# Layer 1's modulation moved from matrix products in layer 0's attention to VectorE row sums in layer 0's MLP

## The chip, the core and the metric

One core of one Trainium2 chip runs the whole program. The metric is the device time of one execution in microseconds; lower is better. All numbers are float32.

## The reference

Two blocks run one after the other on 256 latent tokens of width 1024. The first block has two layers, which also carry 256 context tokens through layer 0. Cut to what matters here:

```python
silu_c, silu_ctx = silu(c), silu(c_ctx)              # 1024 each
for l in range(2):
    mod_lat = silu_c @ w_ada[l] + b_ada[l]           # 1024 x 6144 weights
    mod_ctx = silu_ctx @ w_ada[l] + b_ada[l]
    sh1, sc1, gt1, sh2, sc2, gt2 = split(mod_lat, 6)
    h = rms_norm(x, g_attn[l]) * (1 + sc1) + sh1     # then projections and
    ...                                              # two attentions ("mla", "na")
    x = x + gt1 * gated_merge(...)
    h2 = rms_norm(x, g_mlp[l]) * (1 + sc2) + sh2
    x = x + gt2 * squared_relu(h2 @ w_ff1[l]) @ w_ff2[l]
```

The second block ("hybrid_layer", twice) projects its own norm of x, runs four mixers, and reads a memory `mem` of 256 rows, normed over its width: `rmsnorm(mem, mem_norm_g) @ w_mem_kv`. The memory depends on nothing that the first block computes.

## The kernel before

Features lie on the 128 partitions and tokens in the free dimension, so a 1024 x 256 activation is eight tiles. Each engine has its instructions written out by hand in one order; semaphores join them, and nothing is reordered at run time. Helpers of the same name (`modulation`, `softmax`, `split_weights`) stand once in each engine's block.

**Weights.** `weight_entries` lists every weight tile in the order of use; `weight_chunks` packs them into chunks of up to 2048 columns (1 MB), and SP streams the chunks through `ring`, five slots of 1 MB (L849). Chunks of the merge, output and MLP products are "split": ScalarE writes a rounded high part (L947), VectorE the difference (L1276), into `w_parts`, and TensorE makes three products for each pair of tiles (L427 to L429). Split chunks use ring slots 0 to 2 only, since a buffer of the parts lies over slots 3 and 4; `ring_slots` gives each chunk the slot after the one of the chunk before it, modulo 3 or 5. When a non-split chunk after a split stretch falls in slot 3 or 4, SP waits until TensorE is through with the last split chunk, and all later chunks wait behind it:

```python
if not split and i and slot >= RAW:
    ended = [j for j in range(i) if slots[j][0]]
    if ended:
        sp.wait_ge(*event(*chunk_used(ended[-1])))
```

**Modulation.** The first third of layer 0's is made by TensorE at the start: two columns (silu of c and of c_ctx) are stationary, and 256 columns of w_ada move, 8 products for each of 8 steps (L523), a copy by ScalarE, two transposes, two additions by VectorE. The rest of layer 0's are row sums of VectorE (`row_block`, L1306): w_ada's columns lie on partitions, and a scalar_tensor_tensor over 1024 elements multiplies them with a broadcast silu row (`c_rows`) and accumulates into `mod_sum`; two such instructions, one for c and one for c_ctx, make a block of 128 outputs. All 24 steps of layer 1's modulation are TensorE's, one after every other score tile of layer 0's attention (`modulation_step`, `next_modulation`): each takes one ring chunk.

**Attention.** Layer 0 has four groups of 16 tiles (8 heads times 2 halves): mla and na (512 keys, four key tiles), mlac and nac (context queries, 256 keys, two key tiles), in the order mla, mlac, na, nac. Layer 1 has mla and na only. A tile is a score product (L600), a maximum (L1251), an Exp (L915), a scaling (L1257), transposes (L504), a copy (L909), and for each head, a pair of tiles, a value product (L607). Stages are three tiles apart (AHEAD). In the na group the tiles 4 to 11 also carry the split of h into `h_parts` (ScalarE L1045, VectorE L1282), over 512 tokens in layer 0 and 256 in layer 1, and a bias addition (L1250).

**MLP.** Four groups; in each, eight ff1 tiles and eight ff2 tiles, each 24 products. VectorE takes the relu (L1528), the low part (L1282), the residual (L1492). A weight chunk holds two tiles. Layer 0 moves 512 tokens, layer 1 moves 256. The memory is squared in layer 0's group 1 (its sum on TensorE is L456 between groups 1 and 2), normed in group 2 and multiplied with its gain in layer 1's group 0.

**Block 2** starts with three `memk` tiles (L445), a norm of x, and `dt` (L685), then a long run of projections.

Of the kernel before, what the change touches and what calls it, by code (L numbers as in the profile page):

```python
# [35 lines left out]
ALU = mybir.AluOpType  # L36
# [3 lines left out]
P = 128  # L40
# [31 lines left out]
def weight_entries():  # L72
# [12 lines left out]
    for l in range(L):  # L85
# [17 lines left out]
        for j in range(ADA if l + 1 < L else 0):  # L103
            add(("ada", l + 1, j), "w_ada", l + 1, 0, KT, range(256 * j, 256 * j + 256))
# [98 lines left out]
def program(nc, dram, numbers):  # L203
# [3 lines left out]
    with ctx:  # L207
# [74 lines left out]
        mod_sum = sb("mod_sum", [P, 2, 48])  # L282
# [39 lines left out]
        product = probT[:, :, :, :].rearrange("p a k t -> p a (k t)")  # L322
        c_sig = wide[:, 0:2 * D].rearrange("p (s k) -> p s k", s=2)
# [61 lines left out]

        def modulation_step(l, gi, u):


            if l + 1 < L and u % 2 == 0 and NH * gi + u // 2 <= ADA:
                return NH * gi + u // 2  # L390
            return None
# [5 lines left out]
        def _(pe):  # L397
# [91 lines left out]
            def softmax_attention(tiles, until="y_copied", between=None):  # L489


                for i in range(len(tiles) + AHEAD):
                    if i < len(tiles):
                        g, u, nk, score, _ = tiles[i]
                        ps = next_bank(g, "S", u, until=("exp", g, u))
                        full(score(ps, u), g, "S", u)
                        if between:
                            between(g, u)
# [17 lines left out]
            def modulation(l, j):  # L516


                if j < (ADA if l else FIRST):
# [17 lines left out]
            for l in range(L):  # L537
# [75 lines left out]
                def next_modulation(g, u):  # L613
                    j = modulation_step(l, [name for name, *_ in groups(l)].index(g[0]), u)
                    if j is not None:
                        modulation(l + 1, j)

                softmax_attention([t for g in groups(l) for t in head_tiles(*g[0:7])], between=next_modulation)


# [14 lines left out]
                for g in range(NG):  # L635
# [8 lines left out]
                    if (l, g) == (0, 1):  # L644
                        sum_squares("mem", 2, KT, T)
# [224 lines left out]
        def _(act):  # L870
# [22 lines left out]
            def modulation(l, j):  # L893

                if j < ADA:
# [60 lines left out]
            for l in range(L):  # L956
# [79 lines left out]
                def with_tile(g, u):  # L1036
                    j = modulation_step(l, [name for name, *_ in groups(l)].index(g[0]), u)
                    if j is not None:
                        modulation(l + 1, j)
# [35 lines left out]
                for g in range(NG):  # L1075
# [7 lines left out]
                    for n in range(KT):  # L1083
                        split_weights(("ff2", l, g, n), l)
                        if (l, g) == (0, 1):
# [3 lines left out]
                    if (l, g) == (0, 1):  # L1089
# [116 lines left out]
        def _(dve):  # L1206
# [86 lines left out]
            row_next = {"at": 2 * FIRST}  # L1293

            def row_block():

                b = row_next["at"]
                row_next["at"] = b + 1
                i = place["row", 0, b // 2][0]
                w = ring[:, slots[i][1], D * (b % 2):D * (b % 2) + D]  # L1300
                if b % 2 == 0:
                    dve.wait_ge(*event(f"weights_in{slots[i][1]}", i))
                if b > 2 * FIRST:
                    dve.wait_ge(*event("row_used", b - 1))
                for s in range(2):
                    ins = dve.scalar_tensor_tensor(product[:, s, :], w, 1.0, c_rows[:, s, :], ALU.mult, ALU.mult,  # L1306
                                                   accum_out=mod_sum[:, s, b:b + 1])
                ins.then_inc(*signal("row_used", b))
                seen[("chunk_used", i)] = ("row_used", b)
# [17 lines left out]
            for l in range(L):  # L1327
# [18 lines left out]
                dve.wait_ge(*event("mod", l, (ADA if l else FIRST) - 1))  # L1346
# [17 lines left out]
                def row_blocks(n):  # L1364
                    for _ in range(n if l == 0 else 0):
                        row_block()
# [66 lines left out]
                if l == 0:  # L1433

                    dve.wait_ge(*event("row_used", 47))
                    dve.tensor_tensor(mod(l, 1)[:, 2 * FIRST:48], mod_sum[:, 1, 2 * FIRST:48], p("b_ada", l)[:, 2 * FIRST:48],
                                      ALU.add).then_inc(*signal("late_mod", 1))
                    dve.wait_ge(*event("late_mod", 1))
                    then(dve.tensor_tensor(mod(l, 0)[:, 2 * FIRST:48], mod_sum[:, 0, 2 * FIRST:48], mod(l, 0)[:, 2 * FIRST:48],
                                           ALU.add))  # L1440
# [10 lines left out]
                def with_tile(g, u):  # L1451
                    j = modulation_step(l, list(place_y).index(g[0]), u)
                    if j is not None:
                        modulation(l + 1, j)
# [67 lines left out]
                for g in range(NG):  # L1522
                    for n in range(GT * g, GT * g + GT + 1):
                        if n < GT * g + GT:
# [3 lines left out]
                            dve.tensor_scalar(r, bank(("ff1", l, n))[:, 0:cw], 0.0, None, ALU.max).then_inc(*signal("relu", l, n))  # L1528
                        if n > GT * g:
                            v = (n - 1) % GT  # L1530
                            low_part(b_parts, v, given("raw", ("ff", l, n - 1))[:, t0:TT], slice(t0, TT), "b", "ff", l, g)
                    for n in range(KT):
                        split_weights(("ff2", l, g, n))
                        residual(n, 40, "x_mlp", "ff2", l, g, n)
                        if (l, g) == (0, 1) and n > 1:
                            add_square("mem", 2, n - 1, T)
                        if (l, g) == (0, 2):
# [4 lines left out]
                        if (l, g) == (1, 0):  # L1542
# [205 lines left out]
def lay_out(a):  # L1748
# [55 lines left out]
    return {"w": w, "par": par, "c_rows": np.ascontiguousarray(np.broadcast_to(cvec[None], (P, 2, D))), "bias": bias, "mem": feature_major(a["mem_2"][0]),  # L1804
# [63 lines left out]
```

## Time and profile before

| what | value |
|---|---|
| median of 3 runs | 2325.98 us (2325.98 to 2326.09) |
| the profiled execution | 2324.49 us |
| its span, first to last instruction | 2322.7 us |
| mean granted TensorE clock | 0.983 of full |
| TensorE matmul busy | 2208.5 us (95%) |
| VectorE busy | 1021.5 us (44%) |
| ScalarE busy | 740.7 us (32%) |
| share of TensorE in the chain that ended last | 84% |

The difference between the profiled execution and its span, 1.8 us, is launch and end. Shares are averages over stages with different limits. Matmul records overlap, as products are pipelined: the pitch from one start to the next tells the cost, not the length of one.

### The profile page before, as it was taken

How to read it: one execution, taken by the hardware profiler on the slowest of the kernel's cores; microseconds unless marked ns; L12 is line 12 of the kernel's file. 1: busy time of each engine (PE TensorE's matmuls, PEld its weight loads, DVE VectorE, ACT ScalarE, POOL GpSimd, SP SyncE). 2: the span in 40 equal slices, each digit the busy share in tenths (PEclk: the TensorE clock that was granted, in tenths of full speed). 3: DMA queues.
4: the chain of work that ended last, by engine and by line, in shares of the span. 5: the costliest groups of instructions: out<-in, count | busy, mean ns of one | idle time of the engine just before them, and what ended most of it. 6: DMA issues, size and time to landing. Idle time of an engine off the chain costs nothing.

```text
span 2322.7 us, 26119 instructions
## 1 busy us (share of the span) xinstructions
PE 2208.5 (95%) x10264; PEld 1638.6 (71%) x10264; DVE 1021.5 (44%) x2001; ACT 740.7 (32%) x1379; POOL 2.4 (0%) x8
## 2 busy tenths in 40 slices
PE   7999999999998999999999998999999999999997
PEld 2445334448876888887565488999888788888776
DVE  2555543554445443443235656655440351521342
ACT  3123233343434233232243455444211240201330
POOL 0000000000000000000000000000000000000000
PEclk9999999999999999999999999999999999999999
DMA  7432353313222222223212035445344223434221
GB/s 300 138 133 96 118 198 139 109 55 109 91 91 73 91 98 87 106 73 120 87 36 91 1 134 184 174 177 181 137 161 148 82 109 109 145 136 145 82 91 55
DMA packets 38744, 272.48 MB, mean 117 GB/s; under 512 B 4192, under 2 KB 5344, under 8 KB 7520
## 3 DMA queue, kind: packets, MB, share of 16 engines
q1 hardware_dynamic: 38048, 263.66, 31.5%
q0 software_dynamic: 576, 7.14, 0.8%
q8 instruction: 84, 1.38, 0.2%
q14 instruction: 36, 0.29, 0.0%
HBM read 269.74 MB, written 1.05 MB: 117 GB/s over the span
## 4 chain that ended last, share of the span: by engine, by line
PE 84%; DVE 6%; ACT 6%; issue 4%; DMA 0%; SPq 0%; ACTq 0%; DVEq 0%
PE bank L445 30%; PE bank L427 10%; PE bank L428 10%; PE bank L429 10%; PE bank L481 5%; PE bank L523 5%; PE bank L607 3%; PE bank L600 3%; ACT w_parts L947 2%; PE bank L456 2%; PE bank L504 1%; DVE probT L1306 1%; DVE w_parts L1276 1%; DVE stat L1251 1%; PE bank L677 1%
## 5 line engine op out<-in xcount | busy, mean ns | idle before, releaser
L445 PE MATMUL bank<-h,ring 128*128 128x256 f32 (+2 forms) x2032 | 538.3, 424 | 7.1 <-ACT h L984 7.0
L445 PEld LDWEIGHTS bank<-h,ring 128*128 128x128 f32 (+1 forms) x2032 | 384.7, 191 | 147.8 <-issue 102.2
L1276 DVE TENSOR_TENSOR w_parts<-ring,w_parts 128x2048 fp32r<-128x2048 f32 x96 | 219.9, 2292 | 155.0 <-ACT w_parts L947 154.9
L427 PE MATMUL bank<-h_parts,w_parts 128*128 128x512 f32 (+1 forms) x768 | 263.9, 344 | 15.8 <-DVE h_parts L1519 8.3
L427 PE MATMUL bank<-b_parts,w_parts 128*128 128x512 f32 (+1 forms) x768 | 260.1, 339 | 10.3 <-DVE b_parts L1282 8.8
L428 PE MATMUL bank<-h_parts,w_parts 128*128 128x512 f32 (+1 forms) x768 | 261.1, 340 | 0.0
L429 PE MATMUL bank<-h_parts,w_parts 128*128 128x512 f32 (+1 forms) x768 | 260.6, 339 | 0.0
L428 PE MATMUL bank<-b_parts,w_parts 128*128 128x512 f32 (+1 forms) x768 | 259.0, 337 | 0.0
L429 PE MATMUL bank<-b_parts,w_parts 128*128 128x512 f32 (+1 forms) x768 | 258.9, 337 | 0.0
L947 ACT ACTIVATE w_parts<-ring 128x2048 fp32r<-128x2048 f32 x96 | 182.8, 1906 | 180.1 <-PE bank L429 180.1
L427 PEld LDWEIGHTS bank<-h_parts,w_parts 128*128 128x128 f32 x768 | 147.5, 192 | 38.9 <-issue 17.3
L427 PEld LDWEIGHTS bank<-b_parts,w_parts 128*128 128x128 f32 x768 | 146.4, 191 | 27.6 <-issue 12.4
L429 PEld LDWEIGHTS bank<-h_parts,w_parts 128*128 128x128 f32 x768 | 148.1, 193 | 15.4
L428 PEld LDWEIGHTS bank<-h_parts,w_parts 128*128 128x128 f32 x768 | 148.0, 193 | 14.8
L428 PEld LDWEIGHTS bank<-b_parts,w_parts 128*128 128x128 f32 x768 | 146.4, 191 | 15.2
L429 PEld LDWEIGHTS bank<-b_parts,w_parts 128*128 128x128 f32 x768 | 146.3, 191 | 15.2
L481 PE MATMUL bank<-ring,h 128*128 128x256 f32 x640 | 144.5, 383 | 0.0
L481 PEld LDWEIGHTS bank<-ring,h 128*128 128x128 f32 x640 | 122.7, 192 | 24.7 <-issue 8.7
L523 PE MATMUL bank<-ring,silc 128*2 128x256 f32 x512 | 118.0, 385 | 12.9 <-DMA ring<-in_w 12.9
L915 ACT ACTIVATE prob<-bank,stat 128x512 f32<-128x512 f32 (+1 forms) x112 | 66.8, 596 | 133.6 <-DVE stat L1251 133.5
L523 PEld LDWEIGHTS bank<-ring,silc 128*2 128x2 f32 x512 | 41.4, 85 | 89.4 <-issue 32.1
L600 PE MATMUL bank<-wide 96*128 96x512 f32 (+3 forms) x192 | 94.5, 578 | 0.0
(197 smaller groups left out, 2365.8 us busy)
## 6 DMA issues: line engine op xcount, KB each, us to landing
ring<-in_w SPq DMA_DIRECT2D x237, 1024.0 KB, 4.8
lowrank<-in_bias POOLq DMA_DIRECT2D x2, 2048.0 KB, 9.7
ring<-in_w SPq DMA_DIRECT2D x4, 864.0 KB, 4.6
x<-in_x SPq DMA_DIRECT2D x1, 2048.0 KB, 8.6
ring<-in_w SPq DMA_DIRECT2D x4, 512.0 KB, 3.2
lowrank<-in_con POOLq DMA_DIRECT2D x1, 1856.0 KB, 8.5
ring<-in_w SPq DMA_DIRECT2D x2, 800.0 KB, 4.4
ring<-in_w SPq DMA_DIRECT2D x2, 640.0 KB, 7.8
```

What stands on the lines that cost most here:

```text
L427: pe.matmul(ps, w_hi[:, k, :], hi, start=k == 0, stop=False)
L428: pe.matmul(ps, w_hi[:, k, :], lo, start=False, stop=False)
L429: mm = pe.matmul(ps, w_lo[:, k, :], hi, start=False, stop=k == nk - 1)
L445: mm = pe.matmul(out, w[:, k, :], src(k), start=first and k == 0, stop=last and k == nk - 1)
L456: mm = pe.matmul(ps[:, 0:w], stationary, given("sq", (name, l, k))[:, 0:w], start=k == max(0, n - 2), stop=k == n - 1)
L481: mm = pe.matmul(ps[:, 0:256], src(k)[:, P * t:P * t + P], w[:, k, :], start=k == 0, stop=k == KT - 1)
L523: mm = pe.matmul(ps[0:2, 0:256], silc[:, 2, 2 * k:2 * k + 2], w[:, k, :], start=k == 0, stop=k == KT - 1)
L600: return pe.matmul(ps[:, 0:P * nk], qs[r, a, q:q + P], ks[r, a, 0:P * nk], start=True, stop=True)
L607: mm = pe.matmul(ps[r:r + VD, 0:T], vs[:, k, VD * hd:VD * hd + VD], probT[:, hd % 2, k, :], start=k == 0, stop=k == nk - 1)
L915: act.activation(e[:, 0:w], bank((g, "S", u))[:, 0:w], ACT.Exp, bias=stat[:, u % 4, 0:1], accum_out=stat[:, u % 4, 1:2]).then_inc(*signal( ...
L947: act.activation(w_parts[pair][:, 0, 0:size], ring[:, slot, 0:size], ACT.Copy).then_inc(*signal("w_hi", i))
L1276: dve.tensor_tensor(w_parts[pair][:, 1, 0:size], ring[:, slot, 0:size], w_parts[pair][:, 0, 0:size].bitcast(F32), ALU.subtract).then_inc(* ...
```

## The change

1. The 24 `ada` chunks of layer 1 leave the ring. A new DRAM array `rows` holds w_ada of layer 1 with output columns on partitions, 24 pieces of 1 MB; the GpSimd queue loads them alternately into the two halves of `lowrank` (`rows1`), the first two when layer 0's last output tile is done, each later one when the piece before last has been read.
2. Layer 0's attention has no products between its tiles, neither the copies nor the transposes and additions that belonged to them.
3. VectorE makes 48 row blocks in layer 0's MLP: five in each group's ff1 tiles, seven in its ff2 tiles. `late_modulation(1)` adds the bias before layer 1's first norm. The unused full product of a block is written into the attention's `prob` buffers.
4. `c_rows` is needed until the end of layer 0's MLP, and the memory is loaded into its place after that, behind layer 1's bias on the GpSimd queue. Its squares move to layer 1's group 0, its norm to group 1, its gain to group 2.
5. With 24 chunks fewer, `ring_slots` gives other slots to all later chunks.

```diff
-        for j in range(ADA if l + 1 < L else 0):
-            add(("ada", l + 1, j), "w_ada", l + 1, 0, KT, range(256 * j, 256 * j + 256))
+        product1 = prob_all[:, :, :].rearrange("p (a b) t -> p a (b t)", a=2)
+        rows1 = lowrank[:, :].rearrange("p (a k) -> p a k", a=2)
...
-                softmax_attention([...], between=next_modulation)
+                softmax_attention([...])
...
-                    if (l, g) == (0, 1):
+                    if (l, g) == (1, 0):
                         sum_squares("mem", 2, KT, T)
...
-                if l == 0:
-                    pool.wait_ge(*event("row_used", 47))
-                    pool.dma_start(mem, dram["mem"]).then_inc(*signal("mem_in", by=16))
+                for j in range(ADA if l == 0 else 0):
+                    if j == 0:
+                        pool.wait_ge(*event("psum_full", "out", l, KT - 1))
+                    if j > 1:
+                        pool.wait_ge(*event("row_used", 1, 2 * j - 3))
+                    pool.dma_start(rows1[:, j % 2, :], dram["rows"][j]).then_inc(*signal(f"rows1_in{j % 2}", j, by=16))
+            pool.wait_ge(*event("row_used", 1, 47))
+            pool.dma_start(mem, dram["mem"]).then_inc(*signal("mem_in", by=16))
...
+            def late_modulation(l):
+                dve.wait_ge(*event("row_used", l, 47))
+                late = slice(0 if l else 2 * FIRST, 48)
+                dve.tensor_tensor(mod(l, 1)[:, late], mod_sum[:, l, 1, late], p("b_ada", l)[:, late],
+                                  ALU.add).then_inc(*signal("late_mod", l))
+                dve.wait_ge(*event("late_mod", l))
+                then(dve.tensor_tensor(mod(l, 0)[:, late], mod_sum[:, l, 0, late], mod(l, 0)[:, late], ALU.add))
...
+                        if l == 0 and n < GT * g + GT and n % GT in (0, 1, 3, 4, 5):
+                            row_block(1)
                         if n > GT * g:
                             v = (n - 1) % GT
                             low_part(b_parts, v, ...)
                     for n in range(KT):
                         split_weights(("ff2", l, g, n))
                         residual(n, 40, "x_mlp", "ff2", l, g, n)
-                        if (l, g) == (0, 1) and n > 1:
+                        if l == 0 and n < 7:
+                            row_block(1)
+                        if (l, g) == (1, 0) and n > 1:
                             add_square("mem", 2, n - 1, T)
-                        if (l, g) == (0, 2):
+                        if (l, g) == (1, 1):
...
-                        if (l, g) == (1, 0):
+                        if (l, g) == (1, 2):
```

## Rows read from the trace of the kernel before

**Rows 1.** The head of the page and its busy times.

```profile
span 2322.7 us, 26119 instructions
...
PE 2208.5 (95%) x10264; PEld 1638.6 (71%) x10264; DVE 1021.5 (44%) x2001; ACT 740.7 (32%) x1379; POOL 2.4 (0%) x8
```

**Rows 2.** Windows: nac without products between, then layer 0's MLP.

```profile
core 0: us, PE busy (x) PEld busy (x) DVE busy (x) ACT busy (x) POOL busy (x), PEclk, DMA share, GB/s
...
496.00:520.00 24.00, 22.74 (x93) 10.96 (x92) 14.41 (x50) 12.34 (x44) 0.00 (x0) 1.00 0.00 1
716.00:1074.00 358.00, 353.91 (x1540) 289.75 (x1540) 157.34 (x206) 111.19 (x125) 0.00 (x0) 0.99 0.24 83
```

**Rows 3.** The chain in layer 0's attention: start us, us, what.

```profile
302.06 2.00 PE bank L600 x2
...
333.79 3.55 PE bank L523 x16
...
487.80 1.87 PE bank L607 x8
...
516.24 1.08 PE bank L607 x4
...
524.40 0.64 PE bank L427
```

**Rows 4.** The chain in layer 1's attention.

```profile
1256.59 5.41 PE bank L600 x6
...
1266.51 1.94 PE bank L607 x8
...
1271.64 1.94 PE bank L607 x8
...
1297.80 1.94 PE bank L607 x8
...
1303.40 1.94 PE bank L607 x8
...
1309.31 1.94 PE bank L607 x8
```

**Rows 5.** Groups of instructions: low parts over 256 and over 512 tokens.

```profile
L1282 DVE TENSOR_TENSOR h_parts<-h,h_parts 128x256 fp32r<-128x256 f32 x7 | 3.0, 425 | 2.8 <-ACT h_parts L1045 2.8
...
L1282 DVE TENSOR_TENSOR b_parts<-probT,b_parts 128x512 fp32r<-128x512 f32 x32 | 21.9, 683 | 3.1 <-ACT b_parts L1082 3.1
```

**Rows 6.** The line of the row blocks: duration ns min/median/max, start us.

```profile
L1306 DVE SCALAR_TENSOR_TENSOR probT<-ring,c_rows x64: 1208/1221/1226, 65.6 to 294.2; 128x1024 f32<-128x1024 f32 x64
```

**Rows 7.** VectorE in order of time, ff2 tiles of layer 0: start us, us.

```profile
864.11 0.48 DVE L1492 SCALAR_TENSOR_TENSOR x<-bank,mod_ctx,x 128x256 f32<-128x256 f32 x1 [3.86 <-PE bank L429]
...
866.12 2.29 DVE L1276 TENSOR_TENSOR w_parts<-ring,w_parts 128x2048 fp32r<-128x2048 f32 x1 [1.13 <-ACT w_parts L947]
869.55 0.48 DVE L1492 SCALAR_TENSOR_TENSOR x<-bank,mod_ctx,x 128x256 f32<-128x256 f32 x1 [1.14 <-PE bank L429]
```

**Rows 8.** TensorE and ScalarE around the memory's sum in layer 0's MLP.

```profile
898.10 1.10 PE L456 MATMUL bank<-sq,con 128*128 128x256 f32 x4 [1.39 <-DVE sq L1227]
...
900.13 1.90 ACT L947 ACTIVATE w_parts<-ring 128x2048 fp32r<-128x2048 f32 x1
```

**Rows 9.** The start of block 2 in order of time.

```profile
1645.82 22.04 SPq L849 DMA_DIRECT2D ring<-in_w  x7
...
1650.88 5.38 PE L445 MATMUL bank<-x,ring 128*128 128x256 f32 x16 [5.14 <-issue]
...
1656.09 1.03 PE L456 MATMUL bank<-sq,con 128*128 128x256 f32 x4
...
1656.95 7.07 PE L445 MATMUL bank<-x,ring 128*128 128x256 f32 x32
...
1663.86 3.63 PE L685 MATMUL bank<-ring,h 128*128 128x8 f32 x32
```

**Rows 10.** DMA issues: KB each, median us to landing.

```profile
c_rows<-in_mem POOLq DMA_DIRECT2D x1, 1024.0 KB, 13.9
```

More of the change, by code:

```diff
@@ L487, in values, with softmax_attention @@
                         value_tile(name, l, lw, src, i, t)
-            def softmax_attention(tiles, until="y_copied", between=None):
+            def softmax_attention(tiles, until="y_copied"):
                 for i in range(len(tiles) + AHEAD):
@@ L611, in head_tiles @@
                     return [((gname, l), u, nk, score, value) for u in range(2 * NH)]
[L613 to L618, printed above, removed]
+                softmax_attention([t for g in groups(l) for t in head_tiles(*g[0:7])])
                 for g in groups(l):
@@ L1036, in with_tile @@
                 def with_tile(g, u):
-                    j = modulation_step(l, [name for name, *_ in groups(l)].index(g[0]), u)
-                    if j is not None:
-                        modulation(l + 1, j)
                     if g[0] == "na" and u == 4:
@@ L1291, in _, with row_block @@
                 then(dve.tensor_scalar(gq[:, 2 * i:2 * i + 2], p(name), float(n) ** -0.5, None, ALU.mult))
[L1293 to L1301, printed above, removed]
+            row_next = [2 * FIRST, 0]
+            def row_block(l):
+                b = row_next[l]
+                row_next[l] = b + 1
+                if l:
+                    w = rows1[:, b // 2 % 2, D * (b % 2):D * (b % 2) + D]
+                    dve.wait_ge(*event(f"rows1_in{b // 2 % 2}", b // 2))
+                else:
+                    i = place["row", l, b // 2][0]
+                    w = ring[:, slots[i][1], D * (b % 2):D * (b % 2) + D]
+                    seen[("chunk_used", i)] = ("row_used", l, b)
                     dve.wait_ge(*event(f"weights_in{slots[i][1]}", i))
-                if b > 2 * FIRST:
-                    dve.wait_ge(*event("row_used", b - 1))
+                if b > (0 if l else 2 * FIRST):
+                    dve.wait_ge(*event("row_used", l, b - 1))
                 for s in range(2):
[L1306 to L1309, printed above, removed]
+                    ins = dve.scalar_tensor_tensor((product1 if l else product)[:, s, :], w, 1.0, c_rows[:, s, :], ALU.mult, ALU.mult,
+                                                   accum_out=mod_sum[:, l, s, b:b + 1])
+                ins.then_inc(*signal("row_used", l, b))
+            def late_modulation(l):
[5 more added lines that the diff above has]
+                then(dve.tensor_tensor(mod(l, 0)[:, late], mod_sum[:, l, 0, late], mod(l, 0)[:, late], ALU.add))
             def modulation(l, j):
@@ L1345, in _ @@
                         modulation(0, j)
-                dve.wait_ge(*event("mod", l, (ADA if l else FIRST) - 1))
+                if l == 0:
+                    dve.wait_ge(*event("mod", l, FIRST - 1))
+                else:
+                    late_modulation(1)
                 def gains(which, g):
@@ L1433, in _ @@
                 if l == 0:
[L1435 to L1440, printed above, removed]
+                    late_modulation(0)
                     gains(1, "g_mlp")
@@ L1451, in with_tile @@
                 def with_tile(g, u):
-                    j = modulation_step(l, list(place_y).index(g[0]), u)
-                    if j is not None:
-                        modulation(l + 1, j)
                     if g[0] == "na" and 4 <= u < 4 + KT:
@@ L1803, in lay_out @@
     bias = np.ascontiguousarray(bias.reshape(L, NH, 2, P, T).transpose(0, 3, 2, 1, 4)).astype(np.float32)
-    return {"w": w, "par": par, "c_rows": np.ascontiguousarray(np.broadcast_to(cvec[None], (P, 2, D))), "bias": bias, "mem": feature_major(a["mem_2"][0]),
+    rows = np.ascontiguousarray(np.stack([
+        block(("row",), "w_ada", 1, 0, KT, range(256 * j, 256 * j + 256)) for j in range(ADA)]))
+    return {"w": w, "par": par, "rows": rows, "c_rows": np.ascontiguousarray(np.broadcast_to(cvec[None], (P, 2, D))), "bias": bias, "mem": feature_major(a["mem_2"][0]),
             "x": feature_major(np.concatenate([a["ctx"][0], a["x"][0]])), **constants()}
```

18 lines of the change are left out of this document (6 added, 12 removed).

## The prediction

> **What bounds the kernel now.** I read the page first, then the chain of waits, then the windows stage by stage, and last the order of time where two stages meet. The page says that TensorE is busy for 95% of the span and VectorE for 44% [rows 1], so work that leaves TensorE can be a gain and work that VectorE takes on can be hidden, if it falls where VectorE has room. The chain through layer 0's attention is almost all TensorE: between its own tiles stand the products of layer 1's modulation, 3.55 us each [rows 3], 24 of them, 85 us in all. Layer 1's attention has no such products, and there the chain alternates between TensorE, the maximum on VectorE, the Exp and the copy on ScalarE; the reader sees in it what layer 0's attention falls back to once the products are gone [rows 4]. Layer 0's MLP is TensorE's alone: 353.91 of 358 us, while VectorE works 157.34 us [rows 2]. At the start of block 2 TensorE stands for 5.14 us before its first tile, and this tile comes about 5 us after SP was let go [rows 9]: a weight transfer that could not be issued earlier.
>
> **Part 1: attention of layer 0.** It takes from its first score product to the first product of the merge, 302.06 to 524.40, 222.3 us [rows 3]. I build the same stretch without the modulation from pitches that the trace has, counted from value product to value product. From first score to first value product: 1256.59 to 1266.51, 9.9 us [rows 4]. Five more head pitches in mla at 5.13 us (1266.51 to 1271.64) [rows 4], 25.7. The nac group already runs without products between but for its first pair: from the value product before its eight pitches to the last of them, 487.80 to 516.24, 28.4 us [rows 3]. The mlac group does the same work on the same shapes, so I take 28.4 for it too. In na, layer 1 shows 5.60 us for a head (1297.80 to 1303.40) and 5.91 with the split of h (1303.40 to 1309.31) [rows 4]. Two pitches at the start of na carry value products of two key tiles, 1.08 against 1.94 us [rows 3, 4], so 4.74 each, 9.5; four carry the split over 512 tokens where layer 1 has 256. A low part over 512 costs 683 ns against 425 [rows 5], twice in a pitch, partly beside waits, and I add 0.4 of the 0.52: 6.3 each, 25.2; two at 5.60, 11.2. Na is 45.9. The end is as now, 516.24 to 524.40, 8.2 us. The sum is 9.9 + 25.7 + 28.4 + 45.9 + 28.4 + 8.2 = 146.5, and the saving 222.3 - 146.5 = **75.8 us**. This is less than 85 us, since waits of the softmax that the products covered come to light.
>
> The bounds: if the longer split hides (1.6 us) and the four four-key value products inside the openings of two-key groups do too (4 x 0.86 = 3.4), the saving is 80.8. If na opens at 5.60 (1.7 less), the split costs its full 0.52 and a ScalarE share as large as what I left out (1.0 less), and mlac's heads of 96 rows run half way between nac's mean pitch of 3.55 and mla's 5.13 (8 x 0.79 = 6.3 less), it is 66.8.
>
> Here the clock matters. In the stretch of nac without products between, TensorE was granted 1.00, its 2.4 GHz level [rows 2], and TensorE there still works 22.74 of 24 us, so short waits between tiles did not bring it down. The Trainium skill, in "TensorE: Matmul & The Clock Gate", section "Part 1: The HAM clock gate", says that activity releases the throttle and that idling brings back half speed, which would make the removed products a cover for the clock. By that rule the attention could lose its gain, and it is one of the rivals below; the trace speaks for the full level.
>
> **Part 2: 48 row blocks in layer 0's MLP.** A block is two instructions of 1.22 us [rows 6] and a short accumulator read that the pair partly hides, about 2.5 us; 48 are 120 us. VectorE would work 157 + 120 = 277 of 358 us, 77% [rows 2]. What counts is whether the weight split comes too late behind a block, since VectorE takes instructions in order. In ff2, tile ends lie 5.44 us apart (864.11 to 869.55), and the split starts at 866.12, 2.0 after the residual's start, and takes 2.29 [rows 7]. Its chunk is first needed two tile ends after 864.11, one chunk being two tiles: at 875.0. With a block behind the residual (two halves, 0.9 us), the split starts at 864.1 + 0.9 + 2.5 = 867.5 instead of 866.1 and ends at 869.8, with 5.2 us left. The residual of 869.55 is late by 0.3, and a bank has seven others behind it. Then a block to about 873.2, before the next tile end at 875.0. In ff1 the block of an odd tile fills the time until the high part is ready. No block stands behind tiles 6 and 7 of ff1 or tile 7 of ff2, where the next stage waits for the last low part or residual. So I cost it at **0**. The cover is the 5.2 us; if it were gone, each block would cost its 2.5.
>
> The rows come on the GpSimd queue. Each is needed three tile pitches less one block after its issue, 3 x 5.44 - 2.5 = 13.8 us. The nearest row is the memory's 1 MB, 13.9 us to landing [rows 10]; it was issued right behind a 2 MB transfer in the same queue and had to wait for it, and in the MLP the DMA share is 0.24 [rows 2]. Doubling that share leaves the engines idle half the time. Even 13.9 would be inside the 5.2 of cover. Bounds: 0 and, if one block in each ff1 and ff2 half came late once with its full length, 8 blocks at 2.5 less what the cover takes, at most half, 10 us. For these transfers a rule speaks against the change: the Trainium skill, "SBUF — State Buffer", in "SBUF: two separate sides", warns that VectorE instructions in a two-port mode keep GpSimd from writing its descriptors. That is the rival of late rows below; the rows here do not show such an instruction in the MLP's loop as SBUF to SBUF copies.
>
> Two small additions of `late_modulation(1)` stand beside the sum of squares and the two ScalarE steps of layer 1's norm: nothing.
>
> **Part 3: the memory.** In layer 0 TensorE stood 1.39 us for the last partial sum, and the sum took 1.10 [rows 8]: **2.5 us** go. In layer 1 they come back between groups 0 and 1, and more: ScalarE, in order, must norm the memory before it makes the next high part. In layer 0 this high part began at 900.13, and the tile ended at 898.10 - 1.39 = 896.7 [rows 8], so 3.4 us late. Layer 0 has slack for that. Layer 1's ff1 is a loop of ScalarE and VectorE, since a tile moves half the columns for the same weights to split; a late high part shifts everything after it. So **+3.4**, between 0 and 3.4 + 2.5 = 5.9 if both fall one after the other. The additions, squares and gains in ff2 take the places of the gain that stands there now.
>
> **Part 4: the slots.** Counting chunks: layer 1's split stretch has a fixed 48 chunks as layer 0's has, and 48 is 0 modulo 3. Now the last modulation chunk lies in slot 2, so the split chunks begin in 0 and end in 2, and the next non-split chunk falls in slot 3: SP waits for the end of the MLP. Without the 24 chunks the last one before lies in slot 3, the split chunks begin in slot 1 and end in slot 0, and two non-split chunks go to slots 1 and 2 before the MLP ends. Fifteen non-split chunks in layer 1 keep this for its end. At layer 1's start it gives nothing, as TensorE waits for the norm there. At block 2's start `memk` and `dt` are then at hand. Now from SP's release to `dt` it is 1645.82 to 1663.86, 18.0 us; without the wait and the half clock after it, three tiles at 3.46 (6.91 for two, 1656.95 to 1663.86) and the sum of squares at 0.86 (1656.09 to 1656.95) are 11.2 [rows 9]. The norm of x is ready within that time. So **-6.8**, at least the bare idle time of 5.1 if the mechanism holds.
>
> **The sum.** -75.8 + 0 - 2.5 + 3.4 - 6.8 = -81.7 us on the profiled execution of 2324.5, whose span is 2322.7 with 1.8 around it: 2242.8. The median of the runs lies 1.5 above the profiled time, and from it I get **2244 us**, 3.5% less.
>
> **The rivals.**
>
> *Row blocks reach TensorE (slower).* If the split has no cover after all, for instance because the high part that it waits for also moves, all 48 blocks stand in the path: 120 us more, 2244 + 120 = 2364, slower than before. It decides from 81.7 / 48 = 1.7 us of each block's 2.5 on the path. Against it: 5.2 us of slack in each pair of tiles. 3%.
>
> *Rows come late.* VectorE waits in front of a block and the splits with it. Nothing is lost until a row takes 13.8 + 5.2 = 19 us; at 21 us the 24 rows cost 2 us each, 48, and the time is 2292. The memory row's 13.9 speaks against it. 5%.
>
> *The clock falls in layer 0's attention.* At half clock the score and value products on the chain double. A value product is 1.94 or 1.08; a score product I estimate at 1.0 and 0.5, half of the 2.00 that the first one took [rows 3, 4]. That is 16 x 2.94 for four-key heads and 16 x 1.58 for two-key heads, 72 us, nearly all of part 1's gain: 2316. The 1.00 in the nac stretch is against it. 3%.
>
> *The slots bring nothing,* because another wait (the norm, the memory's gain) takes the place of the transfer: 2244 + 6.8 = 2251. 9%.
>
> *The forecast* keeps 80%. Its own bounds: the low end is -80.8 - 2.5 + 0 - 6.8 = -90.1, 2236; the high end -66.8 - 2.5 + 5.9 - 5.1 + 10 = -58.5, 2267. All high ends together are unlikely; the range that should hold 8 in 10 reaches over the slot rival to 2262.
>
> A measurement of this kernel tells a change from none at about 0.2%, 4.7 us. Faster by more: forecast, slots, late rows, clock (2316 is 0.4% less), 0.96 with a little taken off for late rows beyond 21 us; the same 0.01; slower 0.03.
>
> **What the profile would show.** Part 1: first score product at about 302, first merge product at about 449, value pitches of 5.1, 3.2 to 4, 6.3, granted clock 1.00. Part 2: TensorE busy for about 354 of 358 us in the MLP of layer 0, VectorE about 277; a wait of VectorE for a transfer in front of a row block would show late rows, and a wait of TensorE for the low weight part would show the slower rival. Part 3: a wait of about 1.4 us at layer 1's group 1, and the rest of its MLP some 3 us later than the sum otherwise gives. Part 4: TensorE's first `memk` tile right behind the last ff2 tile. The prediction fails if mlac is bound by something that nac is not, or if VectorE's order lets one late block shift a whole group.

## The result and the profile after

The changed kernel takes **2238.17 us** (median of four runs, 2236.45 to 2240.79) where the kernel before takes 2325.98 (2323.24 to 2326.09): ratio **0.9626 [0.961, 0.9643]**, 3.7% faster. The forecast was 2244 with a range of 2236 to 2262; the time is inside it, 5.8 us below the forecast. The profiled execution took 2238.57 us, its span is 85.9 shorter than before's. The head of its page and its busy times [rows 1]:

```profile
span 2236.8 us, 25368 instructions
...
PE 2112.4 (94%) x9832; PEld 1603.0 (72%) x9832; DVE 1123.3 (50%) x2147; ACT 729.5 (33%) x1355; POOL 15.1 (1%) x32
```

TensorE lost 96 us of work, VectorE took on 102, and the time, 85.9 us shorter, follows TensorE. The windows of four stretches of layer 0's attention and of its MLP show why (columns as in [rows 2]):

```profile
core 0: us, PE busy (x) PEld busy (x) DVE busy (x) ACT busy (x) POOL busy (x), PEclk, DMA share, GB/s
303.00:345.00 42.00, 38.96 (x155) 20.87 (x153) 25.45 (x68) 20.79 (x51) 0.00 (x0) 0.94 0.13 56
345.00:375.00 30.00, 25.39 (x108) 14.12 (x108) 18.92 (x61) 14.04 (x48) 0.00 (x0) 1.00 0.00 1
375.00:420.00 45.00, 39.04 (x157) 18.96 (x156) 32.89 (x79) 24.16 (x58) 0.00 (x0) 1.00 0.00 1
420.00:446.00 26.00, 24.04 (x98) 11.47 (x96) 15.05 (x51) 14.33 (x47) 0.00 (x0) 1.00 0.00 1
638.00:996.00 358.00, 352.24 (x1536) 288.72 (x1536) 263.55 (x388) 109.55 (x119) 11.63 (x22) 0.99 0.43 156
```

In the attention TensorE now pauses for 13 to 15% of the second and third stretch and keeps a granted clock of 1.00. The 0.94 of the first is its opening: the clock is 0.50 between 304 and 306 and 1.00 from 308 on. The kernel before has the same at its opening, 0.50 between 302 and 306, so it is no effect of the change. In the MLP VectorE works 263.55 us instead of 157.34, and TensorE is as busy as before. The chain of layer 0's attention (start us, us, what) answers to [rows 3, 4]:

```profile
303.71 3.73 PE bank L591 x4
...
313.13 1.94 PE bank L598 x8
...
318.27 1.94 PE bank L598 x8
...
338.82 1.94 PE bank L598 x8
...
367.07 1.08 PE bank L598 x4
...
381.38 1.94 PE bank L598 x8
...
386.80 0.53 ACT h_parts L1034
387.35 0.69 DVE h_parts L1271
388.04 0.35 DVE bank L1239
...
406.56 1.94 PE bank L598 x8
...
412.15 1.94 PE bank L598 x8
...
440.44 1.08 PE bank L598 x4
...
448.64 0.77 PE bank L420
```

Read from value product (L598) to value product, each stretch stands beside its forecast: to the first value product 9.4 us (9.9); five mla pitches, 313.13 to 338.82, 25.7 (25.7); mlac, to 367.07, 28.25 (28.4); na, to 412.15, 45.1 (45.9); nac, to 440.44, 28.3 (28.4); the end 8.2 (8.2). In all 144.9 us against 222.3: 77.4 saved, 75.8 forecast.

The MLP of layer 0 on VectorE, in order of time (start us, us, what, idle time before), where a weight split (L1265) stands behind a row block (L1299) [rows 7]:

```profile
789.33 1.22 DVE L1299 SCALAR_TENSOR_TENSOR prob<-lowrank,c_rows 128x1024 f32<-128x1024 f32 x1
...
790.46 1.22 DVE L1299 SCALAR_TENSOR_TENSOR prob<-lowrank,c_rows 128x1024 f32<-128x1024 f32 x1
...
791.61 2.29 DVE L1265 TENSOR_TENSOR w_parts<-ring,w_parts 128x2048 fp32r<-128x2048 f32 x1
793.97 0.48 DVE L1488 SCALAR_TENSOR_TENSOR x<-bank,mod_ctx,x 128x256 f32<-128x256 f32 x1
```

A block takes 2.28 us (789.33 to 791.61). The split ends at 793.9, and its chunk is wanted at the tile end of 799.4, where the next residual begins: 5.5 us are left, where 5.2 were forecast. The whole stretch, from the sum of squares of the MLP's norm to that of layer 1, went from 364.66 us (710.29 to 1074.95) to 362.14 (634.73 to 996.87): -2.5, the memory's sum and nothing for 48 blocks. The rows land in 5.1 us:

```profile
lowrank<-in_rows POOLq DMA_DIRECT2D x24, 1024.0 KB, 5.1
```

In layer 1's MLP the memory's sum and the norm behind it stand at the start of group 1; TensorE, then ScalarE [rows 8]:

```profile
1426.44 1.10 PE L449 MATMUL bank<-sq,con 128*128 128x256 f32 x4 [1.00 <-DVE sq L1216]
```

```profile
1427.64 0.47 ACT L867 ACTIVATE rs<-bank,con 128x256 f32<-128x256 f32 x1 [5.33 <-PE bank L449]
1428.14 0.42 ACT L869 ACTIVATE rs<-rs 128x256 f32<-128x256 f32 x1
1428.47 1.90 ACT L939 ACTIVATE w_parts<-ring 128x2048 fp32r<-128x2048 f32 x1
```

From the last low part of the weights (L1265) of one group to that of the next it was 47.35 us three times before; now it is 49.43 for the group with the norm and 47.34, 47.33 for the others: +2.1, where +3.4 was forecast. The start of block 2 [rows 9]:

```profile
1569.99 3.62 PE L438 MATMUL bank<-x,ring 128*128 128x256 f32 x16
...
1570.23 8.05 SPq L835 DMA_DIRECT2D ring<-in_w  x4
...
1573.44 1.03 PE L449 MATMUL bank<-sq,con 128*128 128x256 f32 x4
...
1574.31 7.07 PE L438 MATMUL bank<-x,ring 128*128 128x256 f32 x32
```

The first `memk` tile starts right behind the last ff2 tile, before SP is let go, and at the full pitch. From the last low part of the weights in the MLP to `dt` it is 31.8 us against 38.8: -7.0, -6.8 forecast.

These are -77.4 - 2.5 + 2.1 - 7.0 = -84.8. Two things that no term spoke of remain. The first score product starts 1.65 us later (303.71 against 302.06). Most of it is there from TensorE's first product on (14.2 against 12.9), and it is chance: the same kernel profiled again, after_again below, starts it at about 302.1, and over all profiles here it lies between 299.5 and 303.7. And the `dt` products with the projections behind them take 101.95 and 100.3 us in the two hybrid layers, against 101.95 and 103.6: -3.3. With both it is -86.5, beside the -85.9 of the spans.

### The profile page after: what moved, and what is told of

It reads as the page before. It is cut to its first block, busy times and chain, and to the rows that moved or that the text cites. A ratio compares the mean times of both kernels' runs of the same rounds, so it can differ in the third digit from the quotient of the medians.

```text
span 2236.8 us, 25368 instructions
## 1 busy us (share of the span) xinstructions
PE 2112.4 (94%) x9832; PEld 1603.0 (72%) x9832; DVE 1123.3 (50%) x2147; ACT 729.5 (33%) x1355; POOL 15.1 (1%) x32
## 3 DMA queue, kind: packets, MB, share of 16 engines
HBM read 269.74 MB, written 1.05 MB: 121 GB/s over the span
## 4 chain that ended last, share of the span: by engine, by line
PE 81%; DVE 7%; ACT 7%; issue 4%; DMA 1%; SPq 0%; ACTq 0%; DVEq 0%
PE bank L438 32%; PE bank L420 10%; PE bank L422 10%; PE bank L421 10%; PE bank L474 5%; PE bank L598 3%; PE bank L591 2%; ACT w_parts L939 2%; PE bank L449 2%; PE bank L514 1%; DVE stat L1240 1%; ACT probT L901 1%; ACT prob L907 1%; DVE probT L1299 1%; DVE w_parts L1265 1%
## 5 line engine op out<-in xcount | busy, mean ns | idle before, releaser
L1265 DVE TENSOR_TENSOR w_parts<-ring,w_parts 128x2048 fp32r<-128x2048 f32 x96 | 219.8, 2291 | 115.1 <-ACT w_parts L939 115.1
L420 PEld LDWEIGHTS bank<-b_parts,w_parts 128*128 128x128 f32 x768 | 146.9, 191 | 27.5 <-issue 12.5
L421 PEld LDWEIGHTS bank<-b_parts,w_parts 128*128 128x128 f32 x768 | 146.9, 191 | 15.1
L1299 DVE SCALAR_TENSOR_TENSOR prob<-lowrank,c_rows 128x1024 f32<-128x1024 f32 x96 | 113.3, 1217 | 0.0
L598 PE MATMUL bank<-probT,wide 128*64 128x256 f32 x320 | 79.3, 387 | 23.1 <-ACT probT L901 22.5
```

The costliest lines, as they stand in the source:

```text
L420: pe.matmul(ps, w_hi[:, k, :], hi, start=k == 0, stop=False)
L421: pe.matmul(ps, w_hi[:, k, :], lo, start=False, stop=False)
L598: mm = pe.matmul(ps[r:r + VD, 0:T], vs[:, k, VD * hd:VD * hd + VD], probT[:, hd % 2, k, :], start=k == 0, stop=k == nk - 1)
L1265: dve.tensor_tensor(w_parts[pair][:, 1, 0:size], ring[:, slot, 0:size], w_parts[pair][:, 0, 0:size].bitcast(F32), ALU.subtract).then_inc(* ...
L1299: ins = dve.scalar_tensor_tensor((product1 if l else product)[:, s, :], w, 1.0, c_rows[:, s, :], ALU.mult, ALU.mult, accum_out=mod_sum[:, ...
```

## The experiments

Each ratio is against the kernel before on the same chip, with its 95% interval. slots_back, slots_only, attn_only and no_blocks ran beside each other (kernel before: 2323.89 us), then blocks_twice, rows_single, mem_later and split_spread (2322.43), then after_again, dt_wide, rows_late_one and all_three (2324.75).

**The slots, undone and alone.** In the changed kernel the first slot is moved so that later chunks fall as they did; in the kernel before it is moved so that they fall as in the changed one, and nothing else is touched.

```diff
 # slots_back: the changed kernel
-    out, last, slot, pair, last_pair = [], {}, -1, 0, {}
+    out, last, slot, pair, last_pair = [], {}, 3, 0, {}
 # slots_only: the kernel before
-    out, last, slot, pair, last_pair = [], {}, -1, 0, {}
+    out, last, slot, pair, last_pair = [], {}, 0, 0, {}
```

> The changed kernel with the ring's first slot shifted so that all chunks from the split stretch on lie in the slots that they had before the change. Slot theory: SP must again wait for the end of layer 1's MLP, TensorE stands about 5 us for the first memk tile and runs its first tiles at half clock; from the last ff2 product to dt it is 18 us instead of 11, so 6.8 us more than the changed kernel, about 2245. Rival (the gain at block 2's start comes from the moved memory norm): no difference, 2238.

> The kernel before with nothing changed but the ring's first slot, shifted by one. Slot theory: block 2 starts 6.8 us sooner, 2326 - 6.8 = 2319.2. Rival (the gain needs the rest of the change): 2326.

Measured: slots_back 2243.68 us, 0.9654 [0.9641, 0.9667]; slots_only 2317.36 us, 0.9974 [0.9965, 0.9983]. Block 2's start in slots_back, then in slots_only:

```profile
1567.79 16.11 SPq L835 DMA_DIRECT2D ring<-in_w  x6
...
1572.63 6.60 PE L438 MATMUL bank<-x,ring 128*128 128x256 f32 x16 [4.92 <-issue]
```

```profile
1645.46 3.62 PE L445 MATMUL bank<-x,ring 128*128 128x256 f32 x16
...
1645.70 14.98 SPq L849 DMA_DIRECT2D ring<-in_w  x5
```

The wait of about 5 us behind SP's release comes back with the old slots and goes without any change of the work. slots_only gains 6.5 us with one number. Part 4 stands, and its gain has nothing to do with the modulation but for the count of chunks.

**The attention alone.** The kernel before without its 24 modulation chunks and steps, with the old slots; the memory stays in layer 0. Layer 1's modulation is left out (twice the bias stands in its place).

```diff
-        for j in range(ADA if l + 1 < L else 0):
-            add(("ada", l + 1, j), "w_ada", l + 1, 0, KT, range(256 * j, 256 * j + 256))
-            if l + 1 < L and u % 2 == 0 and NH * gi + u // 2 <= ADA:
-                return NH * gi + u // 2
```

> The kernel before without any modulation of layer 1 (its shift, scale and gate are the bias twice over, so its output is not the reference's), the memory still in layer 0's MLP, the slots as before. It has part 1 alone. Theory: the attention stretch of layer 0 is 144.9 us as in the changed kernel, MLP of layer 0 as before, so 2326 - 77.4 = 2248.6. Rival (part of the gain is made elsewhere, for example in the MLP): over 2255.

Measured: 2242.73 us, 0.9653 [0.964, 0.9666]. The attention takes 145.0 us (300.46 to 445.48), the MLP of layer 0 364.7 as before. The attention's share is as in the changed kernel. On this chip -77.4 makes 2246.5, and the median lies 3.8 below. The profiled execution has two differences that are not the attention's: both `dt` stretches, told below, take 100.3 us, together 5.0 less than in the profile of the kernel before, and the attention starts 1.5 sooner. That the median owes its 3.8 to them is likely, not shown.

**The row blocks.** Without the 48 blocks and their 24 transfers (modulation left out again), and with each block made twice:

```diff
 # no_blocks
-                        if l == 0 and n < GT * g + GT and n % GT in (0, 1, 3, 4, 5):
-                            row_block(1)
...
-                        if l == 0 and n < 7:
-                            row_block(1)
...
 # blocks_twice
-                for s in range(2):
+                for again in range(2 if l else 1):
+                    if again:
+                        ins.then_inc(*signal("row_again", b))
+                        dve.wait_ge(*event("row_again", b))
+                    for s in range(2):
...
```

> The changed kernel without layer 1's 48 row blocks and without their 24 transfers (layer 1's shift, scale and gate are the bias twice over, so its output is not the reference's). Cover theory: the blocks cost nothing, the time is that of the changed kernel, 2238, within 1 us, and layer 0's MLP is 362.1 us from sum of squares to sum of squares in both. Rival (blocks partly on the path): faster by what they cost, 3 us or more.

> Each of layer 1's 48 row blocks is computed twice in place, so VectorE has 120 us more in layer 0's MLP: 264 + 118 = 382 of now 358 us. Cover theory: a pair of tiles has 10.9 us and VectorE would need up to 4.9 more than the 9 it now takes in ff2, so the cover of 5.2 us is used up in ff2 and VectorE becomes the bound there: the MLP grows by about 30 to 50 us, 2270 to 2290. Rival (blocks are free wherever they stand, as the weight split is far ahead): under 2245. Rival (no cover): 2238 + 118 = 2356.

Measured: no_blocks 2237.46 us, 0.9627 [0.9614, 0.964], its MLP of layer 0 362.16 us against 362.14 with the blocks: they cost nothing. blocks_twice 2265.26 us, 0.9751 [0.9732, 0.9769], below the 2270 to 2290 that were expected; its MLP takes 387.4 us, +25.2. Its window:

```profile
638.00:1021.00 383.00, 355.56 (x1536) 287.65 (x1536) 372.90 (x581) 108.62 (x118) 11.63 (x22) 0.99 0.42 152
```

VectorE is now the engine that works through (372.90 of 383 us). Of 48 x 2.28 = 109 us of added work 84 were still hidden, and 25 showed. By the ratios the whole time is about 29 us longer, more than the MLP's 25: behind the MLP TensorE is at half clock longer, and the stretch to layer 1's next sum of squares takes 2.0 us more (52.6 against 50.6). The rival of row blocks that reach TensorE is real, at about twice this load.

**The rows' transfers.** A piece is issued later than when the piece before last has been read: after the first of the two blocks of the piece before (rows_late_one), or after both, so that nothing is loaded ahead (rows_single).

```diff
                     if j > 1:
-                        pool.wait_ge(*event("row_used", 1, 2 * j - 3))
+                        pool.wait_ge(*event("row_used", 1, 2 * j - 2))   # rows_late_one
 # rows_single
-                    if j > 1:
-                        pool.wait_ge(*event("row_used", 1, 2 * j - 3))
+                    if j > 0:
+                        pool.wait_ge(*event("row_used", 1, 2 * j - 1))
```

> The changed kernel, but each row is loaded only when the row before it has been used up, not the one before that: nothing is prefetched. A row needs 5.1 us to land and the next block would start 3.0 us after the one before it ended, so VectorE stands some 2 to 3 us in front of each row's first block in ff2. Cover theory (5.2 us until TensorE feels it): no change, 2238 within 1 us. Rival (late rows reach TensorE at once): 24 x 2.3 = 55 us more.

> The changed kernel, but each row is issued one block later: 3.0 + 5.4 = 8.4 us before its use in ff2 instead of 13.9. Loop theory (what cost 15 us when nothing was prefetched is that VectorE, its own block and the 5.1 us transfer form one loop): a transfer of 5.1 fits into 8.4, VectorE does not wait for a row, and the time is that of the changed kernel within 1 us. Rival (a shorter lead costs in proportion): about 8 us more.

Measured: rows_single 2256.15 us, 0.9716 [0.9702, 0.973], the MLP 377.7 us, +15.6, which neither expectation had; by the ratios the whole time is about 20 us longer. The waits of VectorE there (total us, times, longest), and the chain through it:

```profile
DVE prob L1299 <- DMA lowrank<-in_rows: 59.9, 19, 5.1
```

```profile
717.02 2.38 DVE prob L1299 x4
...
722.39 2.30 DVE prob L1299 x4
...
724.97 5.10 DMA lowrank<-in_rows
...
730.10 2.38 DVE prob L1299 x4
732.48 2.21 DVE w_parts L1265
```

VectorE waits 5 us for a row, and 60 us of such waits cost 15.6. The chain shows a loop: block, transfer, block, split, and a second block from which the next transfer starts. Two ff2 tiles take 13.1 us in it (717.02 to 730.10) where they take 10.9 (789.33 to 800.21 in the changed kernel), so VectorE falls behind by 2.2 us per pair. That it first eats the 5.2 of cover in each group, and that only what is beyond reaches TensorE, fits the 59.9 and the 15.6 but is a reading. Part of the 15.6 is clock: after waits of TensorE for `w_parts` the granted clock is 0.50 around 738 and again around 919, together for 6.8 us, which at half speed costs at most 3.4 (an estimate). rows_late_one, formed on this reading, took 2236.3 us, 0.9623 [0.961, 0.9636], its MLP 362.17: the transfer's 5.1 us fit beside the tiles again, no wait for rows is left and nothing is lost.

**The memory's place.** The sum goes behind ff1 tile 0 of layer 1's group 1, the norm behind the high part of tile 2.

```diff
+                        if (l, n) == (1, GT):
+                            sum_squares("mem", 2, KT, T)
...
                         split_weights(("ff1", l, n), l)
+                        if (l, n) == (1, GT + 2):
+                            rms("mem", 2, D, P, T, ("mem_normed", KT - 1))
```

> The changed kernel with the memory's sum of squares one ff1 tile later on TensorE and its norm on ScalarE behind the next high part of the weights, where ScalarE waits anyway. Theory: group 1 of layer 1's MLP takes 47.35 us like the others instead of 49.4, so 2.1 us less, 2236. Rival (the 2.1 us are the sum itself or VectorE's additions): no change, 2238.

Measured: 2239.01 us, 0.9639 [0.9626, 0.9653]. The group with the norm takes 48.20 us instead of 49.43: 1.2 of the 2.1 come back, the sum itself still holds up one tile. The median does not resolve 1.2 us: its interval overlaps that of the changed kernel. Nor does the profiled execution as a whole, whose `dt` stretches took 205.6 us, 3.3 more than in the changed kernel's.

**The split of h.** In layer 0's na group two pieces of `h_parts` stood in one head's pitch, four heads long; here each head gets one, with the last two in nac.

```diff
-                    if g[0] == "na" and 4 <= u < 4 + KT:
-                        low_part(h_parts, u - 4, h[:, u - 4, t0:TT], ...)
+                    k = h_split(l, g[0], u)   # na 5, 7, 9, 11, 13, 15, nac 1, 3
+                    if k is not None:
+                        low_part(h_parts, k, h[:, k, t0:TT], ...)
```

> The changed kernel with layer 0's split of h spread: one of the eight pieces in every other tile of na (tiles 5 to 15) and of nac (1 and 3), where two stood in each head of na. Theory (a piece costs its ScalarE and VectorE time on the chain, 0.35 us, wherever it stands): no change, 2238 within 1. Rival (one in a head hides in the wait that the other tile leaves): up to 2.8 us less, 2235.5.

Measured: 2233.75 us, 0.9621 [0.9607, 0.9634]; the attention takes 141.7 us, 3.3 less, and the rival was right (it had said up to 2.8; the pitch ahead of the four, 5.26 before and 4.74 here, gains 0.5 as well). This is read from the trace: by the ratios the whole time is 1 to 2 us below the changed kernel's, and the intervals overlap. The chain, at two na pitches:

```profile
385.05 1.94 PE bank L604 x8
386.99 1.07 PE bank L597 x2
388.06 0.02 issue
388.08 0.44 DVE bank L1246
...
390.65 1.94 PE bank L604 x8
```

No `h_parts` stands in it, and the last five pitches of na are 5.60 us each, where the four with two pieces were 6.48, 6.36, 6.49 and 5.85, 6.3 on the mean. Of two pieces in a pitch one (0.69 us, at 387.35 in the changed kernel's chain above) stood ahead of the maximum; a single one falls into a pause.

**The `dt` products.** The changed kernel again, for the same chip, and the same with `dt`'s 16 products moving 128 columns of the chunk instead of their own 8 (the result is taken from the 8 that belong to it).

```diff
-                        mm = pe.matmul(ps[:, 8 * t:8 * t + 8], h2[:, k, P * t:P * t + P], w[:, k, :],
+                        mm = pe.matmul(ps[:, P * t:P * t + P], h2[:, k, P * t:P * t + P], wide_w(k),
...
```

> The changed kernel unaltered, as the base for the other three on the same chip. 2238 within 2. If the clock's fall behind the dt products is a matter of the execution and not of the kernel, its two stretches from dt to the end of the projections take 100.3, 101.9 or 103.6 us in this profile, not necessarily as in the first one (101.9 and 100.3).

> The changed kernel with the 16 products of dt moving 128 columns instead of 8 (the 120 others are weights that lie beside them; their sums are not read). Theory (the half-clock stretches behind dt come from its narrow products): TensorE stays at full clock in both layers of block 2, dt costs at most 0.1 us more, and the time falls by what the changed kernel loses there, 0 to 3.4 and on the mean about 1.5 us; its lowest runs hardly change. Rival (the stretches come from something else near it, such as the sum of squares or the norm): the profile still shows some, and the time does not change.

Measured: after_again 2238.44 us, 0.9629 [0.9615, 0.9642]; dt_wide 2236.69 us, 0.9622 [0.9609, 0.9635]. The windows just ahead of `dt` and behind it, first of after_again, then the one behind it in dt_wide:

```profile
1575.00:1579.70 4.70, 4.70 (x25) 4.13 (x23) 4.26 (x14) 0.38 (x1) 0.00 (x0) 1.00 1.00 394
1583.50:1587.50 4.00, 4.00 (x11) 3.19 (x11) 0.41 (x3) 0.62 (x3) 0.00 (x0) 0.50 0.69 248
1587.50:1591.50 4.00, 4.00 (x16) 3.32 (x15) 1.25 (x3) 0.00 (x0) 0.00 (x0) 0.74 0.04 14
```

```profile
1582.60:1586.60 4.00, 4.00 (x20) 3.54 (x20) 0.84 (x4) 0.62 (x3) 0.00 (x0) 1.00 0.70 256
```

Behind the 8-column products the granted clock is 0.50, the 1.2 GHz level, although TensorE counts as busy throughout; behind 128-column ones it is 1.00. Over all profiles of this study `dt` and its projections take 100.3, 101.9 or 103.6 us in a layer, and which of them changes between executions of the same kernel; in the two with wide products it was 100.3 four times in four. With narrow products it was 100.3 in 9 layers of 24, among them both of slots_back and both of attn_only. So the products' width is the likely cause and not a proven one: two profiles are few, and the medians, 1.75 us apart, have overlapping intervals.

The same profile of dt_wide also shows something of the attention. Its attention is the changed kernel's, but takes 146.9 us instead of 145.0. In its na group the clock fell once:

```profile
375.00:390.00 15.00, 12.46 (x50) 5.72 (x48) 11.90 (x27) 8.20 (x19) 0.00 (x0) 1.00 0.00 1
390.00:395.00 5.00, 4.24 (x10) 1.91 (x10) 3.06 (x6) 2.49 (x6) 0.00 (x0) 0.66 0.00 0
```

```profile
390.76 3.51 PE bank L598 x8
```

This value product takes 3.51 us instead of 1.94, and its pitch is 7.76 instead of 6.48: 1.3 of the 1.9 us. In the other eleven profiles without the modulation products the clock is 1.00 from the end of the attention's opening to its last value product.

**All three together,** the split of h spread in layer 1 too (na tiles 4 to 7, 9, 11, 13, 15, so that two of the heads keep a pair), and the memory's sum behind ff1 tile 1:

```diff
-                        if (l, n) == (1, GT):
+                        if (l, n) == (1, GT + 1):
                             sum_squares("mem", 2, KT, T)
...
```

> The changed kernel with the split of h at one piece for each head where there is room (layer 0: tiles 5 to 15 of na and 1 and 3 of nac; layer 1: 4 to 7 and 9 to 15), the memory's sum behind the second ff1 tile of group 1 and its norm behind the next high part, and the wide dt products. Theory: -3.3 for layer 0's split, -0.6 for layer 1's, group 1 of layer 1's MLP at 47.5 us instead of 49.4, dt up to -3.4: 2238 - 3.3 - 0.6 - 1.9 - 1.5 = 2230.7. Rival for the memory (the sum costs on TensorE wherever it stands): group 1 stays at 48.2.

Measured: **2228.55 us**, 0.9586 [0.9573, 0.9599], 9.9 below the changed kernel on the same chip, and the fastest version here; the intervals do not overlap. Its profiled span is 12.4 shorter than after_again's: a start 1.7 earlier, which is chance, 3.3 in layer 0's attention, 0.6 in layer 1's, 1.6 in layer 1's MLP (47.83 us for the group), 5.0 in the `dt` stretches (200.5 against 205.6, after_again's being among the longest seen).

## Why the prediction held

**Part 1** was right in mechanism and to 1.6 us in size. Pitches taken from nac and from layer 1 carried over to 0.2 us in mla, mlac and nac. The first value product (9.4 for 9.9) and na's opening (4.53, 4.52 and 5.26 us, where 4.74, 4.74 and 5.60 were taken) were each a little too long in the sum. The 0.4 for the longer split was right as a number (6.3 us on the mean), but its reading, a cost that the softmax must pay, was not: split_spread shows that it comes from two pieces in one pitch, and goes when each pitch has one.

**Part 2** was right: no_blocks against the changed kernel gives 0.0 us, and the cover was 5.5 us. The statement on late rows was wrong in its form. It put the loss at zero until one transfer takes 19 us. rows_single shows a row that is late on every block: the delay adds up from pair to pair, so a 5.1 us transfer without prefetch already costs 15.6 in the stage. What held was that the transfers themselves (5.1 us, 13.9 taken) lie deep inside the distance of 13.8 us.

**Part 3**: -2.5 in layer 0 was exact. +3.4 in layer 1 measured +2.1. I took the whole lateness of the high part, counted from the tile's end, as a shift of the loop. That the 2.1 are the memory's is shown by attn_only, where the sum is in layer 0 and the group takes 47.35. mem_later moved sum and norm together and got 1.2 back; with the sum one tile further on, in all_three, 0.5 of the 2.1 is left. Which share is the norm's and which the sum's was not separated. Why both cost less than was counted was not tried either; that the high part starts some time after the tile's end in this loop anyway is only argued.

**Part 4**: -6.8, measured -7.0 in the trace, 6.2 between slots_back and no_blocks on one chip (no_blocks has the new slots, and the blocks that it lacks cost nothing), and 6.5 in slots_only. The rival that another wait takes the transfer's place is refuted by all three.

**The miss** is 4.2 us on the profiled execution (2238.6 against 2242.8): 1.6 from the attention, 1.3 from the memory, 0.2 from the slots and 3.3 from the clock behind `dt`, less 1.65 of the later start, together 4.8; 0.6 the other way is spread over the rest. The forecast started from an execution of the kernel before whose two `dt` stretches took 205.6 us, and the one after took 202.3; that was no effect of the change, since the same kernel run again had 205.6. So of the three errors of the model, 3.1 us, all had the same sign, and the 3.3 and 1.65 are chance. The rest of the 5.8 is the step from profile to median: 1.5 up was carried over from before (2242.8 to a rounded 2244), and it was 0.4 down.

**The rivals.** The clock did not fall in the changed kernel's attention behind its opening: 1.00 in the three windows from 345 on, with TensorE pausing 7 to 15%. But the rival is not void: in dt_wide's profile it fell once, in one pitch, and cost 1.3 us. That is one pitch in one profile of twelve, where the rival had every pitch at half clock. The Trainium skill's rule on idling ("TensorE: Matmul & The Clock Gate", "Part 1: The HAM clock gate") would fit that one fall, and shows nowhere else at these pauses. The rival's price was also too low in its own terms. It put one score product of each head on the chain; the chain has one in mla, but most heads have two in mlac and nac (0.63 and 0.43 us) and in na (1.05 each), so by its rule the loss would be about 90 us instead of 72 (an estimate from these rows). The rows did not come late: with VectorE working 74% of the MLP, GpSimd's 1 MB transfers landed in 5.1 us, where SP's take 4.8 over the whole program. The port rule of the Trainium skill ("SBUF — State Buffer", "SBUF: two separate sides") does not show here. It speaks of VectorE's two-port mode, and no run shows whether an instruction of this loop uses that mode, so it is not refuted either.

## What to carry to other kernels

Before costing the removal of filler work, look for the same stage without filler elsewhere in the trace: here its pitches gave the new time to about 1% (146.5 us for 144.9). Work moved to a half-idle engine is free as long as each piece ends before the next thing that the busy engine wants from it; for anything loaded in the same loop, compare the loop's whole round (load, use, release) with the pitch, since a delay per round adds up and a single delay does not. Count buffers over the whole schedule after removing chunks: which slot a chunk falls in was worth 6.5 us here, by one number.

## What the runs showed of the hardware

In 15 of the 24 layers with `dt`'s 16 products of 8 moving columns each, TensorE's granted clock went to half behind them, with the engine counted busy throughout (0.50 in after_again's window 1583.50 to 1587.50). These products take 3.5 us at full clock, up to 4.2 where the fall reaches into them. The fall costs 0, 1.7 or 3.3 us per layer, differently in executions of the same kernel. With 128 moving columns, where the 16 take 3.57 us, it was absent four times in four; a test with more profiles would have to show that the width is the cause.

Pauses of half a microsecond or so in each attention pitch, 13% of the time in all, left the clock at 1.00 in eleven profiles of twelve. In the twelfth, dt_wide, it fell once (0.66 over 390 to 395) and one pitch took 1.3 us more.
